# Earlier x loads for the first MLP, halved mLSTM prologue weights, and layer-1 probabilities normalized before their transpose

## The reference

```python
def banded_attention(q, k, v, max_dist, sinks=None):      # blocks of 128 queries see 256 keys
    s = jnp.where(mask[None, :, None, None], s, -jnp.inf)
    m = jnp.max(s, axis=-1)
    if sinks is not None:
        m = jnp.maximum(m, sk)
    p = jnp.exp(s - m[..., None])
    den = jnp.sum(p, axis=-1)
    if sinks is not None:
        den = den + jnp.exp(sk - m)
    o = jnp.einsum('nbhgqk,nbkhd->nbqhgd', p, vv.astype(jnp.float32))
    o = o / jnp.transpose(den, (0, 1, 4, 2, 3))[..., None]
    ...
    for layer in range(DEPTH):
        if layer % 2 == 0:
            qa, ka, va, oa, logi, logf, qb, kb, vb = ab_project(xp, w_in_ab[j], b_gate_ab[j], pos_p)
            ...   # mLSTM (4 heads) beside 3 dilated window groups (8 heads each), merged
            mix_p = ab_output(h_a, oa, outs, lses, w_out_ab[j])
        else:
            q, k, v = c_project(xp, w_in_c[j], pos_p)          # 16 heads, 2 key/value heads, window 128
            o, _ = banded_attention(q, k, v, WIN_C - 1, sinks_c[j])
            mix_p = o.reshape(xp.shape[0], s_len, OUT_C) @ w_out_c[j]
        xp = layer_norm(ALPHA * xp + mix_p, ln1_g[layer], ln1_b[layer])
        xp = layer_norm(ALPHA * xp + sq_relu_mlp(xp, w_up[layer], w_down[layer]), ln2_g[layer], ln2_b[layer])
```

## Time and profile before

| what | value |
|---|---|
| three runs, us | 3147.3, 3149.15, 3156.35; median 3149.15 |
| profiled execution, us | 3150.46 |
| its span, first to last instruction, us | 3148.9 |
| mean granted clock of TensorE | 0.974 |
| PE busy | 2985.0 us, 95% |
| DVE busy | 1562.3 us, 50% |
| ACT busy | 914.5 us, 29% |
| POOL busy | 195.7 us, 6% |

### The profile page before, as it was taken

How to read it: one execution, slowest core, us unless ns; L and a number is a source line. 1 busy time by engine, 2 the same in 40 slices (tenths; PEclk the granted TensorE clock), 3 DMA queues, 4 the chain that set the end, 5 groups by cost and what they waited for, 6 DMA issues and landing times. The chain is left out here.

```text
span 3148.9 us, 46429 instructions
## 1 busy us (share of the span) xinstructions
PE 2985.0 (95%) x18247; PEld 2631.4 (84%) x18247; DVE 1562.3 (50%) x3249; ACT 914.5 (29%) x1939; POOL 195.7 (6%) x244
## 2 busy tenths in 40 slices
PE   6998899999987999999999998899799999999998
PEld 6997688887876778989989987788688989989987
DVE  4556435435335764454444446555555344444456
ACT  3223324233323343111112114454433111111114
POOL 0000000000001101101101100000001101101100
PEclk9998899999998999999999999899899999999999
DMA  4003512444978762101101112210421111101111
GB/s 142 31 20 97 155 57 92 175 146 166 318 223 307 274 216 75 54 27 53 53 27 53 53 40 77 93 46 24 170 77 41 54 36 45 53 29 51 53 40 70
DMA packets 134425, 300.21 MB, mean 95 GB/s; under 512 B 15048, under 2 KB 63368, under 8 KB 133192
## 3 DMA queue, kind: packets, MB, share of 16 engines
q1 hardware_dynamic: 134280, 298.19, 28.1%
HBM read 260.65 MB, written 93.34 MB: 112 GB/s over the span
## 5 line engine op out<-in xcount | busy, mean ns | idle before, releaser
L2872 DVE TENSOR_TENSOR f_hT_lo<-f_h,f_hT_hi 128x384 fp32r<-128x384 f32 (+1 forms) x192 | 145.6, 758 | 544.7 <-ACT f_hT_hi L2779 541.2
L529 PE MATMUL g_ps_b<-g_w_hi,g_xT_hi 128*128 128x512 f32 x648 | 255.1, 395 | 2.2 <-DVE g_xT_lo L660 2.2
L529 PE MATMUL g_ps_b<-g_w_lo,g_xT_hi 128*128 128x512 f32 (+1 forms) x648 | 251.8, 391 | 0.0
L2856 POOL TENSOR_TENSOR f_h<-f_h 128x384 f32<-128x384 f32 (+1 forms) x192 | 152.9, 796 | 1281.2 <-ACT f_h L2774 1281.0
L529 PE MATMUL g_ps_b<-g_w_hi,g_xT_lo 128*128 128x512 f32 x576 | 225.3, 391 | 0.0
L2702 PE MATMUL wp_ps_t<-f_xT_hi,f_up_hi 128*128 128x384 f32 (+1 forms) x512 | 169.1, 330 | 3.5 <-DVE f_xT_lo L2642 1.9
L2702 PE MATMUL sp_ps_t<-f_xT_hi,f_up_hi 128*128 128x384 f32 (+1 forms) x512 | 169.7, 331 | 2.2 <-DVE f_xT_lo L2642 1.9
L2702 PE MATMUL sp_ps_t<-f_xT_lo,f_up_hi 128*128 128x384 f32 (+1 forms) x512 | 169.3, 331 | 0.0
L2702 PE MATMUL sp_ps_t<-f_xT_hi,f_up_lo 128*128 128x384 f32 (+1 forms) x512 | 169.1, 330 | 0.0
L2702 PE MATMUL wp_ps_t<-f_xT_lo,f_up_hi 128*128 128x384 f32 (+1 forms) x512 | 168.6, 329 | 0.0
L2702 PE MATMUL wp_ps_t<-f_xT_hi,f_up_lo 128*128 128x384 f32 (+1 forms) x512 | 168.5, 329 | 0.0
(11 more groups left out here) (554 smaller groups left out, 7369.3 us busy)
## 6 DMA issues: line engine op xcount, KB each, us to landing
w_group<-in_w_in_ab SPq DMA_DIRECT2D x9, 2048.0 KB, 11.2
sample_keys<-in_w_up SPq DMA_DIRECT2D x16, 1024.0 KB, 7.1
sample_keys<-in_w_down SPq DMA_DIRECT2D x16, 1024.0 KB, 5.0
wo<-in_w_up SPq DMA_DIRECT2D x16, 1024.0 KB, 7.1
wo<-in_w_down SPq DMA_DIRECT2D x16, 1024.0 KB, 5.0
out<-in_cache_dil_kv SPq DMA_DIRECT2D x8, 2016.0 KB
g_xn<-in_x_prompt SPq DMA_DIRECT2D x16, 512.0 KB, 4.2
sample_keys<-in_cache_dil_kv SPq DMA_DIRECT2D x8, 1024.0 KB, 7.7
```

The costliest lines, as they stand in the source:

```text
L529: last = pe.matmul(bank(n, "z", c)[0:w, 0:CHUNKS[c][0]], xp, wp, start=(k == 0 and q == 0), stop=(k == KT - 1 and q == len(passes) - 1))
L2856: pool.tensor_tensor(hs, hs, hs, ALU.mult).then_inc(squared.sem, 1)
L2872: last = dve.tensor_tensor(hT[par][1][:, f, t0:end], hs[:, 0:end - t0], as32(hT[par][0][:, f, t0:end]), ALU.subtract)
```

## The change

Four things. In the mLSTM prologue the weights are split in two halves of k, the orders of PE, ACT and DVE change, and x tile 1 is loaded after chunk 2. In attention "c", DVE multiplies the probabilities by the reciprocal denominator before they are transposed (`scale_probs`); the back transposes and `o_out` go, and o is stored transposed, in a new buffer `mixT_c`. The following projection loads those tiles as they are and transposes only the sample's. In `sample_and_projection`, SP issues the loads of the first MLP's six x tiles and its first weights right behind `load_mix(NT)`.

```diff
@@ mlstm
-                    if c == 1:
+                    if c == 2:
                         load(0, 1)
...
                 def project(n, par, chunks):
                     for c in chunks:
-                        if isinstance(n, int) and n == 0:
-                            pe.wait_ge(w_lo, c + 1)
                         for k in range(KT):
+                            if isinstance(n, int) and n == 0 and k % (KT // 2) == 0:
+                                pe.wait_ge(w_lo, 2 * c + k // (KT // 2) + 1)
...
-                project(0, 0, (0,))
+                project(0, 0, (0, 1, 2))
                 x_transposes(0, -2, 0, 1)
-                project(0, 0, range(1, NCH))
+                project(0, 0, range(3, NCH))
...
-                    nc.scalar.copy(w_high[c][:, :, :], w_raw[c][:, :, :]).then_inc(w_hi, 1)
+                    for ks in halves_of_k:
+                        nc.scalar.copy(w_high[c][:, ks, :], w_raw[c][:, ks, :]).then_inc(w_hi, 1)
...
                 x_out(0, -4, 0)
-                round_weights(0)
-                round_weights(1)
+                for c in range(NCH):
+                    round_weights(c)
                 x_out(0, -2, 1)
-                for c in range(2, NCH):
-                    round_weights(c)
...
                 def rest_of_weights(c):
-                    dve.wait_ge(w_hi, c + 1)
-                    dve.tensor_tensor(w_low[c][:, :, :], w_raw[c][:, :, :], w_high[c][:, :, :].bitcast(F32), ALU.subtract).then_inc(w_lo, 1)
+                    for half, ks in enumerate(halves_of_k):
+                        dve.wait_ge(w_hi, 2 * c + half + 1)
+                        dve.tensor_tensor(w_low[c][:, ks, :], w_raw[c][:, ks, :], w_high[c][:, ks, :].bitcast(F32), ALU.subtract).then_inc(w_lo, 1)
...
                 rest_of_weights(1)
+                z_out(0, 0, (0, 1))
+                rest_of_weights(2)
+                rest_of_weights(3)
+                z_out(0, 0, (2,))
+                rest_of_weights(4)
                 x_rest(0, -2, 1)
-                z_out(0, 0, (0,))
-                for c in range(2, NCH):
-                    rest_of_weights(c)
-                    z_out(0, 0, (c - 1,))
-                z_out(0, 0, (NCH - 1,))
+                z_out(0, 0, (3, 4))
@@ attention
-        oT = sb("oT", [P, PAIRS, P])
+        oT = [sb(f"oT{i}", [P, PAIRS, P]) for i in range(2 if swa else 1)]
...
                 def store_o(n):
+                    if swa:
+                        sp.dma_start(g["out"][n], oT[n % 2][:, :, :].rearrange("p u t -> p (u t)")).then_inc(o_stored[n % 2], 16)
+                        return
...
-                        pe.wait_ge(exp_done, index(n) * PAIRS + (4 * b + 3) // each // 2 + 1)
+                        if swa:
+                            pe.wait_ge(scaled, 2 * n + (4 * b + 3) // each // 8 + 1)
+                        else:
+                            pe.wait_ge(exp_done, index(n) * PAIRS + (4 * b + 3) // each // 2 + 1)
...
-                    if attends(n - 1):
+                    if attends(n - 1) and not swa:
                         back(n - 1)
...
-                    if swa:
-                        act.wait_ge(sk_ready, n + 1)
-                        nc.scalar.activation(sk[:, :], sk[:, :], ACT.Exp).then_inc(sink_done, 1)
+                        if swa and h % 8 == 7:
+                            act.wait_ge(sk_ready, 2 * n + h // 8 + 1)
+                            nc.scalar.activation(sk[:, h - 7:h + 1], sk[:, h - 7:h + 1], ACT.Exp).then_inc(sink_done, 1)
...
+                def scale_probs(n, part):
+
+                    w, o, hs = P * spans(n), osb[n % 2], slice(8 * part, 8 * part + 8)
+                    dve.wait_ge(sink_done, 2 * n + part + 1)
+                    link(dve.tensor_tensor(rden[:, hs], o[:, H + 8 * part:H + 8 * part + 8], sk[:, hs], ALU.add))
+                    link(dve.reciprocal(rden[:, hs], rden[:, hs]))
+                    dve.tensor_tensor(prob[:, hs, 0:w], prob[:, hs, 0:w],
+                                      rden[:, hs].rearrange("p (h o) -> p h o", o=1).broadcast_to([P, 8, w]), ALU.mult).then_inc(scaled, 1)
...
                             maxima(n, 1)
+                            scale_probs(n, 0)
...
                             z_out(n + 1, c)
+                            if swa and c == 1 and attends(n):
+                                scale_probs(n, 1)
@@ window_sample_and_projection
                 def load_mix(n):
-                    sp.dma_start(mixt[n % 2][0:rows_of(n), :], cfg["mix"][n * P:n * P + rows_of(n), :]).then_inc(m_loaded[n % 2], 16)
+                    src = cfg["mixT"][n] if n < NT else cfg["mix"]
+                    sp.dma_start(mixt[n % 2][0:rows_of(n), :], src).then_inc(m_loaded[n % 2], 16)
...
-                    for half in range(2):
-                        pe.wait_ge(*banks.free(n, "m", half))
+                    pe.wait_ge(m_lo, 2 * (n + 1))
...
-                    if n + 2 < NTT:
-                        mix_transposes(n + 2)
+                    if n + 2 == NT:
+                        mix_transposes(NT)
@@ sample_and_projection
                         load_mix(NT)
+                        sp.wait_ge(*banks.full(BD - 1, "o"))
+                        for m in range(6):
+                            load_ahead(m)
+                            if m == 2:
+                                cfg["prefetch"](sp)
...
-                    if n == BD:
-                        sp.wait_ge(*banks.full(BD - 1, "o"))
-                        for m in range(X_AHEAD):
-                            load_ahead(m)
-                            if m == 1:
-                                cfg["prefetch"](sp)
-                    if n == NTT:
-                        for m in range(X_AHEAD, 6):
-                            load_ahead(m)
```

More of the change, by code:

```diff
@@ L424, in _ @@
                         for b in range(HALVES):
-                            sp.wait_ge(*banks.free(n - 1, "back", b))
+                            sp.wait_ge(*banks.free(n - 1, "o" if swa else "back", b))
                         store_o(n - 1)
@@ L510, in back @@
                         pe.wait_ge(*banks.free(n, "o", b))
-                        transposes([oT[:, 4 * b + u, :] for u in range(4)], P, n, "back", b)
+                        transposes([oT[0][:, 4 * b + u, :] for u in range(4)], P, n, "back", b)
                 def project(n, c):
@@ L718, in maxima @@
                         dve.wait_ge(*lo_count(0, 2, 1))
-                    if part == 0 and index(n) >= 2:
+                    if part == 0 and index(n) >= 2 and not swa:
                         dve.wait_ge(o_stored[index(n) % 2], o_count([m for m in range(n) if attends(m)][-2]))
@@ L741, in o_out @@
                 def o_out(n):
-                    o = osb[index(n) % 2]
-                    if not swa:
-                        dve.wait_ge(*banks.full(n, "back", 0))
-                        dve.tensor_copy(o[:, 0:512], bank(n, "back", 0)[:, :]).then_inc(banks.free(n, "back", 0)[0], 1)
-                        return
-                    dve.wait_ge(sink_done, n + 1)
-                    link(dve.tensor_tensor(rden[:, :], o[:, H * DH + H:H * DH + 2 * H], sk[:, :], ALU.add))
-                    link(dve.reciprocal(rden[:, :], rden[:, :]))
@@ L750, in o_out @@
-                    for b in range(HALVES):
-                        dve.wait_ge(*banks.full(n, "back", b))
-                        dve.tensor_tensor(o[:, b * 512:(b + 1) * 512].rearrange("p (h d) -> p h d", d=DH),
-                                          bank(n, "back", b)[:, :].rearrange("p (h d) -> p h d", d=DH),
-                                          rden[:, 8 * b:8 * b + 8].rearrange("p (h o) -> p h o", o=1).broadcast_to([P, 8, DH]),
-                                          ALU.mult).then_inc(banks.free(n, "back", b)[0], 1)
+                    dve.wait_ge(*banks.full(n, "back", 0))
@@ new lines, in o_out @@
+                    dve.tensor_copy(osb[index(n) % 2][:, 0:512], bank(n, "back", 0)[:, :]).then_inc(banks.free(n, "back", 0)[0], 1)
+                def scale_probs(n, part):
[5 more added lines that the diff above has]
+                                      rden[:, hs].rearrange("p (h o) -> p h o", o=1).broadcast_to([P, 8, w]), ALU.mult).then_inc(scaled, 1)
@@ L1565, in uses @@
         for n in range(NTT):
-            for half in range(2):
-                yield (n, "m", half), "t"
+            if n == NT:
+                for half in range(2):
+                    yield (n, "m", half), "t"
             for c in range(2):
@@ L1812, in mix_out @@
                     rows = rows_of(n)
+                    if n >= 2:
+                        act.wait_ge(*banks.full(n - 2, "y", 1))
+                    if n < NT:
+                        act.wait_ge(m_loaded[n % 2], 16 * (n // 2 + 1))
                     for half in range(2):
-                        act.wait_ge(*banks.full(n, "m", half))
-                        nc.scalar.copy(mT[n % 2][0][:, 4 * half:4 * half + 4, 0:rows],
```

(9 more changed lines are left out.)

43 lines of the change are left out of this document (26 added, 17 removed).

## The result

The changed kernel takes 3130.0 us (median of five runs, 3126.3 to 3131.6), against 3149.15 before; the ratio is 0.9935 with an interval of 0.992 to 0.9949. A second series gave 0.9931 (0.9917 to 0.9945). The forecast was 3130.0. Of all executions in this document one, of the last kernel, ran at a mean granted clock of 0.744 and took 3751.14 us; no ratio here contains it. An interval is one of 95%.

What follows compares the result with a forecast made beforehand. PE, busy 2985.0 of 3148.9 us, was taken as the bound. The four parts lie one behind the other on its path, so -4.4 - 8.2 - 1.4 - 5.2 = -19.2 gave 3130.0 us by the median, range 3118 to 3145.

Steps and rivals of the forecast that it cites:

- D: From the sample attention into the first MLP: x tiles and weights asked for earlier, -8.2 us (-5 to -10).
- A: Prologue of the mLSTM: weights in halves let chunk 0 start earlier, -4.4 us (-2 to -7).
- B: Layer-1 attention: back transposes go, scaling is added on DVE, -1.4 us (-5.5 to +4).
- C: Projection of layer 1: mix transposes go in six places at 0.87 each, -5.2 us (-3 to -5.5).
- half prices: Prologue: a half of 3072 columns costs ACT 1.48 and DVE 1.75 us, so chunk 0 starts at 16.15.
- the half clock that I assumed: Prologue, behind the wait ahead of chunk 2: low clock as before, 7.7 us; 2.2 more goes if it stays up.
- rival 2: Queue into the first MLP: at 300 GB/s the sample's x lands at 1177, D is -6.0, total 3132.3; chance 0.10.
- 2.7 + 2.5: Last tile of layer-1 attention: value products 2.7 us later, plus 2.5 (0 to +5) for possible half clock.
- about 6 us: Last tile of layer-1 attention: PE's wait ahead of the last transposes of probabilities grows to this.
- 7.33 of idle time for DVE: Layer-1 attention: DVE idle 2.58 + 4.75 us per tile, so it has room for the scaling; the order decides.
- the 3.5 that it named as a sign: Layer-1 attention: DVE's idle time per tile after the change would be 3.5 us.
- 0 to +2: Start of the layer-1 projection: the low clock may rise later with two fewer transpose groups ahead, 0 to +2 us.

Runs made afterwards that it cites:

- the last kernel: Changed kernel with prologue, x-load and last-tile orders changed together, plus SP storing the last tile's o before the sample's queries, keys and values: 3118.6 us, ratio 0.9898.
- the third order: Changed kernel, but in the mLSTM prologue DVE makes the rest of chunk 2 before it copies out chunk 1: 3123.8 us, ratio 0.9926.
- the kernel with the doubled scaling: Changed kernel with two more DVE instructions of 128x1024 ahead of each scaling, 4.7 us per scaling in place of 2.3: 3158.2 us, ratio 1.0022.

## Why the prediction was right, and where its steps were not

The forecast, direction and mechanism of each part were right. That the total agreed to the microsecond is luck: the interval of the measured change runs from 16 to 25 us, and D alone differs by 2 us from trace to trace. But every term lies in or near what the traces show for it:

| part | forecast | first pair of traces | all traces with the part's code as in the change |
|---|---|---|---|
| A, to the end of the prologue | -4.4 | -4.6 | -4.6 to -5.9 |
| D, to x tile 6 | -8.2 | -5.8 | -5.8 and -5.9 (two), -7.8 to -8.1 (five) |
| B, last tile included | -1.4 | -1.9 | -1.2 to -1.9 |
| C, to the end of the trace | -5.2 | -4.0 | -3.1 to -5.4 |

- **A came out a little larger than forecast.** Each step came: half prices, chunk 0 at 15.94 for 16.15, a wait that stays ahead of chunk 2 (3.01 for 3.3; the prediction's own numbers, 29.05 less 25.85, give 3.2). Behind it the half clock that I assumed came in four of seven traces and stayed away in three, for which the prediction named 2.2 more: these three gain 5.5 to 5.9, the four 4.6 to 5.3. What I had not asked was whether the wait could be had for nothing: `z_out` ahead of `rest_of_weights(2)` is its cause, as the third order shows.
- **D was right, and its rival 2 also happened.** Everything up to the first hidden unit came as worked out (8.3 in every trace with the change, wait 1.63 for 1.6). From SP's first load to the landing of the sample's x the prediction has 19.0 to 20.0 (1155.4 to 1174.4 or 1175.4) and a cost of 0 to 0.6 for DVE. Five traces show 19.5 to 19.8 and a wait of 0.18 to 0.41. Two show 21.4 and 20.9 and a wait of 2.12 and 1.50; DVE's residual, the store and x tile 6 hang on it, and D is 5.8, which is rival 2 (-6.0). Its cause is not the one that I gave. In the first trace the queue moved 377 to 410 GB/s, more than my 347 and far more than the rival's 300, and then stood at a DMA share of 0.19 at 1165 to 1168; as I read it, a few of the engines were still at the last packets. Why only some executions have this is open.
- **B was right by two errors that cancelled.** I counted six tiles with a full stream of work and there are seven, so -5.8 and not -5.1. The last tile lost 5.3 up to the end of the value products, near my 2.7 + 2.5: 3.0 as two waits (1.54 and 3.49, where one of 2.02 was), 1.3 of half clock on twelve transposes and 0.8 on the value products. The end of the tile, for which I gave 1.5, brought 1.4 (15.4 to 16.8). The multiplication took 2.29 for 2.25. The prediction's "about 6 us" of wait doesn't follow from its own 2.02 + 2.7, and its 7.33 of idle time for DVE is not the whole: it is the sum of two waits, while DVE is busy 15.7 of 29.07 us per tile before and 19.5 of 28.23 afterwards, so 8.7 are idle and not the 3.5 that it named as a sign. The forecast didn't rest on that sum but on the times at which PE wants its banks. The Trainium skill, "TensorE: Matmul & The Clock Gate" (section "HAM oscillation — how this bites in real kernels"), describes a loop in which PE waits some 3 to 5 us for data and starts each burst at the half rate. The 3.49 fits that (2.79 for what took 1.50), and the 2.02, which left the clock up, is shorter than those waits. The waits of 3.00 and 3.01 in the prologue show both outcomes.
- **C was somewhat too large.** Six times 0.85 came. Against it stands the clock at the start, which I had as 0 to +2 and set at 0: it is 0.67 in 2237 to 2241 and costs 1.1. In six other traces 1.4 to 1.9 are lost at the start of the last MLP instead, where the clock falls: it is 0.50 behind a wait of 1.93 in the second trace of the changed kernel, and 1.00 behind one of 1.92 in the first. I had said that the chain into the last MLP only moves along.
- **The rest, 4.5 us in the first pair of traces**, is not of these steps, and I had no term for it. 3.2 of it lie between the prologue and attention g, and there they are the first trace's: the three others with the old prologue are 2.6 to 3.1 ahead of it. That trace was not a long one (3150.46, with medians of 3149 to 3151 in five series); the second trace of the kernel before was the shortest of its ten executions (3143.84). With the middle of each range above, the four parts sum to 18 to 19, against 19.1 by the medians and 20.5 by the ratio. So nothing systematic has to be in the rest, though an interval of 16 to 25 can't exclude it.

## What to carry to other kernels

When loads are asked for earlier, write down what now stands behind them in the same queue and when that is wanted, and leave a margin on bytes by mean rate: here the landing agreed with it in five traces and came 1 to 2 us behind it in two. When work moves to an engine with idle time, slack is the time between its slots and the consumer's, not the sum of its idle time, and the last iteration, where the neighbour's work is shorter, needs its own timetable: its order alone cost almost as much as the other tiles' gain. Effects of 5 us in 3150 are read from local steps in aligned traces, and not from the time. And before a local step is explained, look at it in several traces, above all in those of other edits that leave the place alone: from one trace I took a wait of 2.12 for a property of the kernel, and the next five had 0.4 or less.

## What the runs showed of the hardware that I had not expected

The granted clock of the same work in the same kernel differs from execution to execution: 0.50 over the end of the sample's mLSTM in one and 0.89 in the next, 4.0 us between them at that place, and the spans of two executions of one kernel 6.6 us apart, and the local step of D 5.8 and 5.9 in two traces and 7.8 to 8.1 in five. A wait of 3.49 or 3.50 ended in half clock in each of the six traces that have it (2.79 for twelve transposes), and so did one of 2.56 in a tile of the kernel with the doubled scaling; in its next tile, behind a wait of 2.55, they took 1.58 and the clock fell right after them (0.73). The same wait of 3.00 to 3.01 in the prologue brought 0.50 in four traces and left 1.00 in three. How long PE was idle is thus not all that decides.
